# A hybrid decoder step in fp32: three engines' instruction orders changed around the attention heads

## What is computed

```python
def mlstm_chunked(q, k, v, i_pre, f_pre, C0, n0, m0):     # per chunk of 128, per sample group
    s = jnp.einsum('blhd,bshd->bhls', qc, kc) * w_in      # masked, weighted scores
    num = jnp.einsum('bhls,bshv->bhlv', s, vc) + jnp.einsum('blhd,bhdv->bhlv', qc, C) * w_prev[..., None]
    g = exp(log_g - m_new)                                # weights of the keys, from the gates
    C_new = C * decay + jnp.einsum('bshd,bshv->bhdv', kc * g, vc)
def retention_chunked(q, k, v, S0):
    s = jnp.einsum('blhd,bshd->bhls', qc, kc) * intra
    o = jnp.einsum('bhls,bshv->blhv', s, vc) + jnp.einsum('blhd,bhdv->blhv', qc, S) * cross
    S_new = S * chunk_decay + jnp.einsum('bshd,bshv->bhdv', kc * into, vc)
xbc, conv_new = causal_dwconv(xbc, conv0, conv_w, conv_b) # width 4, "taps", feeds the SSD
out = head_norm(o) * gate                                 # then the output projection
```

## Time and profile before

| | |
|---|---|
| Median of three runs | 1037.89 us (1037.03 to 1038.46) |
| Profiled execution, its own time | 1032.65 us |
| Its span, first to last instruction | 1030.9 us |
| TensorE busy | 991.7 us (96%) |
| VectorE busy | 747.9 us (73%) |
| ScalarE busy | 559.2 us (54%) |
| GpSimd busy | 381.0 us (37%) |
| Mean granted clock of TensorE | 0.984 of full speed |

### The profile page before, as it was taken

One profiled execution on the slowest core, in us unless ns is written; L12 is line 12 of the kernel. 1 busy time (PEld: TensorE's weight loads), 2 busy tenths in 40 slices (PEclk: granted clock), 3 DMA queues, 4 the chain that ended last, 5 costly groups with the idle time before them and its releaser, 6 DMA issues.

```text
span 1030.9 us, 19172 instructions
## 1 busy us (share of the span) xinstructions
PE 991.7 (96%) x7256; PEld 939.5 (91%) x7256; DVE 747.9 (73%) x1326; ACT 559.2 (54%) x932; POOL 381.0 (37%) x599
## 2 busy tenths in 40 slices
PE   7989999898899999999999999999999999999996
PEld 6989888777589999999999999899989999999996
DVE  5776788877866999996458857677765699999442
ACT  6536666633544766555444356666645566665431
POOL 4003223224211777772005521322222377777100
PEclk9999999999899999999999999999999999999998
DMA  8463464453555554545444735776635455544541
GB/s 295 140 242 123 129 210 131 153 187 108 168 180 185 173 175 165 164 164 180 163 164 164 266 126 189 219 236 183 206 133 187 161 172 170 169 166 165 179 144 46
DMA packets 64684, 177.22 MB, mean 172 GB/s; under 512 B 5888, under 2 KB 24064, under 8 KB 64592
## 3 DMA queue, kind: packets, MB, share of 16 engines
q1 hardware_dynamic: 64304, 174.86, 51.0%
q0 software_dynamic: 288, 1.12, 0.3%
HBM read 154.92 MB, written 21.05 MB: 171 GB/s over the span
## 4 chain that ended last, share of the span: by engine, by line
PE 85%; DVE 6%; ACT 4%; issue 3%; POOL 1%; DMA 1%; SPq 0%; DVEq 0%; ACTq 0%; POOLq 0%
PE bank L809 25%; PE bank L811 24%; PE bank L810 24%; PE bank L855 2%; ACT wh L1227 2%; DVE wl L1633 1%; PE bank L1165 1%; PE bank L1133 1%; DMA raw<-wts 1%; PE bank L1095 1%; PE bank L867 1%; POOL sts L2353 1%; PE bank L876 1%; PE bank L875 0%; PE bank L1139 0%
## 5 line engine op out<-in xcount | busy, mean ns | idle before, releaser
L1227 ACT ACTIVATE wh<-raw 128x1024 fp32r<-128x1024 f32 x257 | 270.5, 1057 | 318.3 <-PE bank L811 317.6
L1633 DVE TENSOR_TENSOR wl<-raw,wh 128x1024 fp32r<-128x1024 f32 x257 | 321.3, 1254 | 164.4 <-ACT wh L1227 162.4
L809 PE MATMUL bank<-hH,wh 128*128 128x288 f32 x1160 | 352.9, 304 | 7.1 <-DVE wl L1633 4.8
L810 PE MATMUL bank<-hL,wh 128*128 128x288 f32 x1160 | 345.5, 298 | 0.0
L811 PE MATMUL bank<-hH,wl 128*128 128x288 f32 x1160 | 344.3, 297 | 0.0
L809 PEld LDWEIGHTS bank<-hH,wh 128*128 128x128 f32 x1160 | 221.0, 191 | 10.7 <-DVE wl L1633 3.4
L810 PEld LDWEIGHTS bank<-hL,wh 128*128 128x128 f32 x1160 | 221.2, 191 | 0.6
L811 PEld LDWEIGHTS bank<-hH,wl 128*128 128x128 f32 x1160 | 221.5, 191 | 0.0
L1756 DVE SCALAR_TENSOR_TENSOR cy<-pad,vec,cy 128x304 f32<-128x304 f32 (+1 forms) x212 | 139.5, 659 | 4.5 <-ACT cy L1275 0.6
L2194 POOL COPY pad<-fst 128x16 f32<-128x16 f32 x88 | 94.3, 1076 | 67.7 <-DVE cy L1756 67.7
L809 PE MATMUL bank<-upH,wh 128*128 128x288 f32 x352 | 104.4, 297 | 0.0
(11 more groups left out here) (336 smaller groups left out, 1605.7 us busy)
## 6 DMA issues: line engine op xcount, KB each, us to landing
raw<-wts SPq DMA_DIRECT2D x257, 512.0 KB, 3.3
st<-r_in SPq DMA_DIRECT2D x9, 512.0 KB, 6.5
r_out<-st SPq DMA_DIRECT2D x9, 512.0 KB, 4.4
st<-c_in SPq DMA_DIRECT2D x8, 514.0 KB, 6.8
c_out<-st SPq DMA_DIRECT2D x8, 514.0 KB, 5.0
sts<-h_in SPq DMA_DIRECT2D x12, 256.0 KB, 5.1
h_out<-sts SPq DMA_DIRECT2D x12, 256.0 KB, 2.6
st3r<-r_in SPq DMA_DIRECT2D x4, 512.0 KB, 6.0
```

The lines of the kernel that those rows point to most:

```text
L809: mm(out, h, xh, start=(k == 0), stop=False)
L810: mm(out, h, xl, start=False, stop=False)
L1227: s.do(act(wh[:, c % RING, :], raw[:, c % RING, :], ACT.Copy), hi_ready)
L1633: do(tt(wl[:, c % RING, :], raw[:, c % RING, :], wh[:, c % RING, :].bitcast(F32), ALU.subtract), lo_ready)
```

## The change

Three places, none of which adds or removes work. `gate_exponentials` on ScalarE and `gate_slab` on VectorE move two tiles later. ScalarE's `keys` moves ahead of the weight split of the head's last tile, in the mLSTM heads and in the retention heads. In the mLSTM heads VectorE does the taps of tile t + 1 not ahead of the split of step t + 3, but behind the samples' output and the first four updates.

```diff
@@ ScalarE, first projection
-                if t == GATES + 4:
+                if t == GATES + 6:
                     gate_exponentials()
@@ ScalarE, mLSTM head h
                 product(f"asp{h}", pout[:, h % 2, 0:AV + 1])
-                step_a(t + 3)
                 if h + 1 < AH:
                     keys("a", h + 1, h + 1)
+                step_a(t + 3)
@@ ScalarE, retention head h
+                if h + 1 < CH:
+                    keys("r", h + 1, hg + 1)
                 step(h, 3)
                 if h:
                     inverse(hg - 1)
-                if h + 1 < CH:
-                    keys("r", h + 1, hg + 1)
@@ VectorE
-            def step_a(t):
+            def step_a(t, taps=True):
...
-                if TILES[t - 2][1] == "xbc" and t - 2 >= T0:
-                    convolve_x(TILES[t - 2][2])
+                if taps:
+                    taps_of(t - 2)
                 split(place(t, 0)[0] + 3)
+
+            def taps_of(t):
+
+                if TILES[t][1] == "xbc" and t >= T0:
+                    convolve_x(TILES[t][2])
...
-                if t == GATES + 5:
+                if t == GATES + 7:
                     gate_slab()
...
-                step_a(t + 3)
+                step_a(t + 3, taps=False)
                 sample_out_a(h)
                 updates_a(h, range(4))
+                taps_of(t + 1)
```

## The result

The changed kernel is slower: 1050.77 us median of five runs (1048.77 to 1051.34), against 1037.89 us for the kernel before (1033.93 to 1038.46). The ratio is 1.0131, 95% interval 1.0112 to 1.0150. The prediction was 1047.8 us, in the range of 1039 to 1055. The sign and the place were right.

A forecast was written before the change was run, and what follows sets the result against it. TensorE, busy 96% of the span, was taken as the bound. Gates -3.2, mLSTM -3.8, retention delay +11.8 and clock +5.1 gave +9.9 us, added to the 1037.89 us median: 1047.8 us, 8-in-10 range 1039 to 1055.

The forecast's parts named there:

- Gates, -3.2 forecast: Gates: later exponentials let the splits start on time, removing TensorE's wait for the value tile; gain 3.2 us.
- the three tiles of lead: Gates: each weight split runs three tiles ahead, 3.2 us per tile, which hides the moved exponentials.
- mLSTM, -3.8 forecast: mLSTM heads: keys gain 4.1 us, moved taps cost 2.0, one clock dip fewer gains 1.7; sum -3.8 us.
- 0.8 and 1.2 us of waits: mLSTM: waits added by moved taps at the passages from head 0 to 1 and 1 to 2.
- VectorE's full stretch: mLSTM head 3: VectorE is full from 171 to 193 us, so the third passage's added wait vanishes there.
- the rule's 3.8 us: mLSTM: by the exclusive lock, taps lose the full 1.9 us at each passage, making added waits 3.8 us.
- both sums: mLSTM: two prices for the moved taps' added waits, 2.0 us as forecast and 3.8 by the lock rule.
- my 2.0: mLSTM: forecast total of waits the moved taps add at two passages, 2.0 us.
- the 2.72 us of head 3: mLSTM head 3: wait for `num` falls to 1.1 us, but TensorE waits again at 193.6; counted as nothing.
- Retention, the delay, +11.8 forecast: Retention: late split delays normalising; TensorE waits 1.9 us in heads 1 to 6, 0.4 in head 0; 11.8 us.
- Retention, the clock, +5.1 forecast: Retention: the new waits bring three clock dips in six heads, costing 5.1 us (bounds 0 and 10.2).
- A dip in every retention head: Rival, retention: the clock dips in every head, +5.1 us more, giving 1052.9 us; chance 18%.

The follow-up runs named there:

- experiment 3: Kernel before with only the gate exponentials and gate slab two tiles later: 1030.68 us, ratio 0.9956.
- 5: Kernel before with the gates' edit and the earlier mLSTM keys, without moved taps or retention step: 1027.53 us, ratio 0.9914.
- experiment 2: Kernel before with only the retention heads' keys moved ahead of ScalarE's split: 1057.8 us, ratio 1.0217.
- 4: Kernel before with only the last mLSTM taps moved behind the first four updates: 1038.06 us, ratio 1.0017.
- experiment 6: Changed kernel, retention: ScalarE's inverse ahead of the keys, VectorE's split behind value copies, scores and normalising: 1026.55 us, ratio 0.9909.
- experiment 7: Changed kernel with nine unused matmuls ahead of the waiting transposes in retention heads 1 to 6: 1039.54 us, ratio 1.0033.

## Why the prediction was right, and where it wasn't

**Gates, -3.2 forecast.** Right: -3.2 at L957, and -4.0 by medians alone, whose interval holds it. A chunk did come late, though: ScalarE stands for 3.82 us until 61.96 for weights that have not landed, and in experiment 3 for 3.91. In the kernel before it has no such wait in this stretch. The state loads may be the cause; no run tells. TensorE has no wait there, so the three tiles of lead hid it, and the gain was what I counted.

**mLSTM, -3.8 forecast.** The table has -3.1 from L957 to the SSD's start, by other terms than mine. The keys gave their waits as counted: none for `kgs` is left. How much of them reaches the SSD is less sure: from experiment 3 to 5 the stretch gets 3.0 us shorter, with one dip fewer in it. The moved taps were mis-sized: I counted 0.8 and 1.2 us of waits, and they have 0.99, 1.61 and 1.74, 4.3 us. Both priced passages were too cheap, and the third, which I thought would vanish in VectorE's full stretch, has its wait too. In heads 0 to 2 the taps took 1.73, 1.95 and 1.78 us more than 1.69, beside `kgm` of 1.90, 1.89 and 2.01. The trace thus agrees with the exclusive lock of the Trainium skill (SBUF — State Buffer, "SBUF: two separate sides"). On the waits the rule's 3.8 us lie nearer to the 4.3, but by luck: at the two passages that both sums price, the waits are 2.6 us, nearer to my 2.0. The split behind the taps, which both sums priced at 1.2 us, no longer meets `kgm` and takes 1.21 to 1.28.

What made up for the taps: the 2.72 us of head 3, which I counted at nothing, went, and VectorE took 2.8 back at L875, as the argument on its full stretch had it.

Of dips I counted two before the change, and there are three: head 3 has one as well, behind its wait of 2.72 us (0.85, 0.50 and 0.80 from 184 to 190). The one of head 1 went, as forecast, and the last got twice as long, from 182 to 192: the clock loses 5.1 us from 90 to 196 in both traces, though after the change 0.7 of it or so falls into the wait at L875. The rows of waits alone (-4.1 - 2.7 + 4.3 + 2.8) would come to +0.3. From start to start the same places, with a wait of head 2 for `Sp` that also goes, come to -1.2. With the 0.7 that makes -1.9, and the other 1.2 of the -3.1 I can't assign.

**After it, nothing forecast.** The SSD gave back 1.0 us (-6.3 to -5.3). TensorE's wait for ScalarE's `xbcT` at L1095 is 3.4 us in two instances, before 2.4 in one. All six experiments with the gates' edit in them, experiment 3 with this edit alone too, have 3.3 or 3.4 in two; both without it (2 and 4) have 2.4 or 2.5 in one. So it comes with the gates' edit. That a hidden wait shows up because the work ahead got shorter is a guess.

**Retention, the delay, +11.8 forecast.** Right, link by link and in size: 3.6 us idle ahead of `kg`, split behind `kgs`, six delays of 1.91 us where 1.9 was forecast, and 0.5 in head 0 where it was 0.4.

**Retention, the clock, +5.1 forecast.** **This is the step that failed:** three dips in six heads, where the trace has seven lengths of one, 10.9 us. I took the share of dips from waits in the mLSTM heads, two in three, and went below it. With head 3's, which I overlooked, it is three in four. And the retention heads repeat one pattern to 0.02 us before the change, so that all or none was the likelier guess. "A dip in every retention head" stood as a rival, 1052.9 us with 18%, and is what came true.

In the traces the sum was thus +9.9 forecast against +17.7: 5.8 short by the clock, 1.0 by the SSD, 0.7 by the mLSTM, 0.2 by the delay, and 0.1 by rounding. That the median was met to 3.0 us has a second reason, which was luck: the profiled execution of before lay 5.2 us under its median, and I added that difference; the profiled execution of after lies 0.4 us under its own. The kernel before took from 1032.2 to 1039.4 us in all its executions, the changed one from 1048.8 to 1051.3 in five. Whether it really scatters less, and why, stays open; traces of kernels that share a stretch differ there by a dip or two.

Open stays why head 2 has a low stretch of double length (661 to 668 us) in the trace of after; its waits are those of the others. In experiment 2 it is head 1 that has it (647 to 654), so the length doesn't belong to one head.

## What to carry to other kernels

Ahead of moving an instruction, look at what is queued behind everything that it delays, on each engine in turn: here the moved keys hold ScalarE's split, that holds VectorE's, and behind it stood the one result that TensorE had 0.9 us of slack for. The split itself could be late at no cost (experiment 6). Where a place repeats exactly, price a dip of TensorE's clock in every repetition and in none, ahead of anything between: here it came in all six heads or, without the wait, in none. Delay and clock cost about the same, and useless matmuls in the wait won the clock's half back (experiment 7).

## What the runs showed of the hardware

- TensorE's clock fell to its lower level after a delay of 1.9 us (1.48 idle, in two pieces), in a stretch of small products and transposes between two tiles (0.77 us busy in the 2 us from 636). In all six places it stayed low for about 3.4 us at a cost of 1.7 us of work, in one of them for twice that. With nine matmuls of 128x288 in the wait it stayed at 1.00.
- Three taps of 1.69 us took 3.42, 3.64 and 3.47 us when GpSimd's `kgm` (1.90, 1.89 and 2.01 us) fell into them. Splits of 1.22 us that met it took 2.41 to 2.89. VectorE's updates with an operand in PSUM were not held: in the retention heads of the kernel before, 14 of 128x512 lie wholly beside a `kgm` and took 680 to 683 ns, the 18 others 679 to 690. The updates of the earlier trace rows don't show it against `kgm`, since none of them ran beside it.
